# Ending a data-dependent loop over expert slots: an earlier branch, down products inside gate and up, and another waiter for the last scatter

## The reference, cut to what matters

```python
def _moe(h, router_w, router_bias, w_gate, w_up, w_down):
    ...
    _, idx = lax.top_k(masked, TOP_K)
    w = jnp.take_along_axis(scores, idx, axis=-1)
    w = w / jnp.sum(w, axis=-1, keepdims=True)
    comb = jnp.sum(jax.nn.one_hot(idx, N_EXPERTS, dtype=jnp.float32) * w[..., None], axis=1).astype(h.dtype)
    y = jnp.zeros_like(h)
    for e in range(N_EXPERTS):
        he = jax.nn.silu(h @ w_gate[e]) * (h @ w_up[e])
        y = y + comb[:, e:e + 1] * (he @ w_down[e])
    return y

def reference(...):
    for i in range(DEPTH):
        ...
        x = x + g1 * yx
        hx = _rmsnorm(x, norm_ffn[i]) * (1 + sc2) + sh2
        ...
        x = x + g2 * y.reshape(b, l, d)
    return x
```

## Time and profile before

| | us |
|---|---|
| runs before: lowest, median, highest | 1151.88, 1154.61, 1158.58 |
| span of the profiled execution | 1154.3 |
| PE busy | 1078.6 (93% of the span) |
| DVE busy | 802.1 (69%) |
| ACT busy | 480.6 (42%) |
| POOL busy | 178.4 (15%) |
| DMA, mean over the span | 211 GB/s |
| granted TensorE clock, mean | 0.976 of full |

### The profile page before, as it was taken

One profiled execution on the slowest core, in us unless ns is written; L12 is line 12 of the kernel. 1 busy time (PEld: TensorE's weight loads), 2 busy tenths in 40 slices (PEclk: granted clock), 3 DMA queues, 4 the chain that ended last, 5 costly groups with the idle time before them and its releaser, 6 DMA issues.

```text
span 1154.3 us, 14887 instructions
## 1 busy us (share of the span) xinstructions
PE 1078.6 (93%) x4739; PEld 793.5 (69%) x4739; DVE 802.1 (69%) x966; ACT 480.6 (42%) x662; POOL 178.4 (15%) x135
## 2 busy tenths in 40 slices
PE   4999999899999999589999999999999999999992
PEld 2554456577777776268888888878887677777771
DVE  5886996788988887356345435454575788988881
ACT  5211224276676765431111111132232366676760
POOL 2101111122232232100000000000000123323331
PEclk9989999999999999889999999999999899999996
DMA  9878649677979973603733223313134888999742
GB/s 366 316 270 316 255 190 416 226 247 205 330 241 320 342 231 75 238 21 125 273 110 115 74 103 127 127 38 145 73 132 161 342 271 262 353 337 297 227 97 43
DMA packets 82002, 243.48 MB, mean 211 GB/s; under 512 B 10016, under 2 KB 34808, under 8 KB 72700
## 3 DMA queue, kind: packets, MB, share of 16 engines
q1 hardware_dynamic: 62436, 188.88, 43.3%
q0 software_dynamic: 17920, 48.31, 16.5%
q10 hardware_dynamic: 1560, 5.26, 1.3%
HBM read 218.29 MB, written 40.89 MB: 225 GB/s over the span
## 4 chain that ended last, share of the span: by engine, by line
PE 76%; DVE 11%; DMA 6%; issue 3%; ACT 2%; SPq 0%; POOL 0%; DVEq 0%; ACTq 0%; POOLq 0%
PE PS L1944 21%; PE PS L1822 8%; PE PS L2047 7%; PE PS L2051 7%; PE PS L2048 7%; PE PS L1957 6%; PE PS L1963 5%; PE PS L1934 4%; DVE ACC L1133 3%; PE PS L1673 3%; PE PS L1635 2%; DMA WAE<-in_w_ada_dram 2%; PE PS L1837 1%; DMA x_dram<-YO,TOKI 1%; DMA SLAB<-in_w_ada_dram 1%
## 5 line engine op out<-in xcount | busy, mean ns | idle before, releaser
L1454 DVE TENSOR_TENSOR WL<-RAW,WH 128x1024 fp32r<-128x1024 f32 x192 | 225.4, 1216 | 0.2
L927 ACT ACTIVATE WH<-RAW 128x1024 fp32r x184 | 184.6, 1052 | 35.1 <-issue 25.2
L2047 PE MATMUL PS<-HTH,WINH 128*128 128x512 f32 x384 | 150.9, 393 | 5.6 <-DVE HTL L1554 5.3
L1944 PE MATMUL PS<-WH,XTH 128*128 128x512 f32 x368 | 147.3, 400 | 5.5 <-issue 5.5
L2048 PE MATMUL PS<-HTL,WINH 128*128 128x512 f32 x384 | 150.0, 391 | 0.0
L1944 PE MATMUL PS<-WH,XTL 128*128 128x512 f32 x368 | 144.1, 392 | 0.0
L1944 PE MATMUL PS<-WL,XTH 128*128 128x512 f32 x368 | 143.5, 390 | 0.0
L2051 PE MATMUL PS<-HTH,WINL 128*128 128x512 f32 x384 | 118.8, 390 | 0.0
L1957 PE MATMUL PS<-WDR,HETF 128*128 x184 | 87.9, 600 | 5.7 <-DVE YO L1468 4.9
L1468 DVE SCALAR_TENSOR_TENSOR YO<-PS,WOF,ROWS 128x1024 f32<-128x1024 f32 x46 | 59.0, 1284 | 42.3 <-PE PS L1963 35.1
L2047 PEld LDWEIGHTS PS<-HTH,WINH 128*128 128x128 f32 x384 | 72.3, 188 | 22.3 <-DVE HTL L1554 4.8
(11 more groups left out here) (244 smaller groups left out, 1723.7 us busy)
## 6 DMA issues: line engine op xcount, KB each, us to landing
RAW<-in_moe_w_gate_dram SPq DMA_DIRECT2D x32, 1024.0 KB, 6.9
RAW<-in_moe_w_up_dram SPq DMA_DIRECT2D x32, 1024.0 KB, 10.9
WDR<-in_moe_w_down_dram SPq DMA_DIRECT2D x32, 1024.0 KB, 10.0
WA<-in_w_ada_dram SPq DMA_DIRECT2D x28, 1024.0 KB, 7.8
WAE<-in_w_ada_dram SPq DMA_DIRECT2D x12, 1024.0 KB, 8.9
WINR<-in_conv_w_in_dram SPq DMA_DIRECT2D x24, 512.0 KB, 3.9
SLAB<-in_w_ada_dram SPq DMA_DIRECT2D x8, 1024.0 KB, 12.3
X<-x_dram SPq DMA_DIRECT2D x16, 512.0 KB, 5.7
```

The lines of the kernel that those rows point to most:

```text
L927: nc.scalar.activation(piece_of(WH[par], i), raw_piece(at, i), ACT.Copy).then_inc(w_high, 1)
L1454: V.tensor_tensor(piece_of(WL[par], i), raw_piece(e, i), piece_of(WH[par], i).bitcast(f32), ALU.subtract).then_inc(w_low, 1)
L1944: ins = T.matmul(bank(2), x[:, ch, :], w[par][:, :, ch, :], start=ch == 0 and i == 0, stop=ch == NC - 1 and i == 2)
L2047: T.matmul(bank(b), WINH[par][:, ch, :], HTH[:, ch, cols], start=ch == 0, stop=False)
```

## The change

The deciding branch is asked before the last two slots instead of after them. `ending(i, used)` takes the place of `slots_from`: slots 1 to 13 are always run, and if `used > 2 * i`, slots 2i-2 and 2i-1 run in their usual form. Otherwise `closing(2i-2)`, `last(2i-1)` and a `drain` that only evens out the semaphores. In the closing slot TensorE has the down product of slot n-3 between the two halves of gate and up, and in the last slot that of slot n-2. The last slot rounds no weights for a slot that does not come, and prepares its own down weights before its silu. POOL makes two gathers fewer in each layer. The last scatter of a layer counts on a semaphore of its own, `last_scattered`, SyncE waits for that, and POOL waits for no landing after it. Core of the diff, in the order SyncE, POOL, ScalarE (`last`), VectorE (`closing`, `last`), TensorE; `ending` is TensorE's and has the same shape on the other engines:

```diff
-                sp.wait_ge(moe_done, 1)
+                sp.wait_ge(last_scattered, 16)
...
-        sp.wait_ge(moe_done, 2)
+        sp.wait_ge(last_scattered, 32)
...
         def drain(layer, n):
-            scatter(layer, n - 2)
-            scatter(layer, n - 1)
-            pool.wait_ge(y_scattered[layer], 16 * n)
-            for par in range(2):
-                pool.wait_ge(gathered[layer][par], (min(n + 2, MAX_SLOTS) + 1 - par) // 2 * 16)
+            scatter(layer, n - 2, y_scattered[layer])
+            scatter(layer, n - 1, last_scattered)
             pool.sem_inc(y_added, MAX_SLOTS - n + 1)
...
+            def last(s):
+                xt_high(s)
+                down_weights(s - 1)
+                down_high(s, down_loaded(s))
+                gate(s)
+                hidden_high(s)
...
+            def closing(s):
+                before, after = expert_of(s - 1), expert_of(s + 1)
+                xt_low(s)
+                y_evac(s - 2, s % 2)
+                weights_low(s + 1, (s + 1) % 2, after, (0,))
+                het_split(s - 1)
+                down_low(s - 1, before)
+                weights_low(s + 1, (s + 1) % 2, after, (1, 2))
+                y_evac(s - 1, 1 - s % 2)
+                weights_low(s + 1, (s + 1) % 2, after, (3,))
+                gated(s, s % 2)
+
+            def last(s):
+                before, at = expert_of(s - 1), expert_of(s)
+                xt_low(s)
+                het_split(s - 1)
+                down_low(s - 1, before)
+                y_evac(s - 1, 1 - s % 2)
+                down_low(s, at)
+                gated(s, s % 2)
+                het_split(s)
+                y_evac(s, s % 2)
...
+            def gate_up_around_down(s):
+                pe.wait_ge(he_ready, s + b0)
+                hidden_transposes(s - 1, 1 - s % 2)
+                gate_up(s, s % 2, range(NC // 2))
+                down_of(s - 1, expert_of(s - 1))
+                gate_up(s, s % 2, range(NC // 2, NC))
+
+            def closing(s):
+                transposes(s, s % 2, s // 2 + 1)
+                down_of(s - 2, expert_of(s - 2))
+                gate_up_around_down(s)
+
+            def last(s):
+                transposes(s, s % 2, s // 2 + 1)
+                gate_up_around_down(s)
+                at = expert_of(s)
+                pe.wait_ge(he_ready, s + b0 + 1)
+                hidden_transposes(s, s % 2)
+                down_of(s, at)
...
-            def slots_from(i, used):
+            def ending(i, used):
+                if i > LAST_STEP:
+                    slot(2 * i - 2)
+                    closing(2 * i - 1)
+                    last(2 * i)
+                    drain(MAX_SLOTS)
+                    return
                 with pe.If(used > 2 * i):
-                    for s in slots_of(i):
-                        slot(s)
-                    if i < LAST_STEP:
-                        slots_from(i + 1, used)
-                    else:
-                        drain(MAX_SLOTS)
+                    slot(2 * i - 2)
+                    slot(2 * i - 1)
+                    ending(i + 1, used)
                 with pe.Else():
+                    closing(2 * i - 2)
+                    last(2 * i - 1)
                     drain(2 * i)
```

More of the change, by code:

```diff
@@ L655, in gather, with scatter @@
                                     ).then_inc(gathered[layer][par], 16)
-        def scatter(layer, s):
+        def scatter(layer, s, done):
             pool.wait_ge(yo_ready, s + (layer * MAX_SLOTS + 1))
@@ L714, in _ @@
             pool.wait_ge(x_stored[layer], 16 * NT)
-            for s in range(2 * ALWAYS):
+            for s in range(2 * ALWAYS - 2):
                 slot(layer, s)
-            slots_from(layer, ALWAYS, used)
-            pool.sem_inc(moe_done, 1)
+            ending(layer, ALWAYS, used)
             if layer == 0:
@@ L980, in _ @@
             nc.scalar.activation(SG[:], bank(2)[:, 0:FF], ACT.Silu).then_inc(silu_g, 1)
-            for s in range(1, 2 * ALWAYS):
+            for s in range(1, 2 * ALWAYS - 2):
                 slot(s)
-            slots_from(ALWAYS, used)
+            ending(ALWAYS, used)
             if layer == 0:
@@ L1493, in drain, with ending @@
                         dve.sem_inc(sig, MAX_SLOTS - n)
[L1494 to L1504 removed]
+                    dve.sem_inc(w_low, PIECES * (MAX_SLOTS - n))
+            def ending(i, used):
+                if i > LAST_STEP:
+                    slot(2 * i - 2)
+                    closing(2 * i - 1)
+                    last(2 * i)
+                    drain(MAX_SLOTS)
+                    return
+                with dve.If(used > 2 * i):
+                    slot(2 * i - 2)
+                    slot(2 * i - 1)
+                    ending(i + 1, used)
                 with dve.Else():
+                    closing(2 * i - 2)
+                    last(2 * i - 1)
                     drain(2 * i)
@@ L1993, in drain, with ending @@
                         pe.sem_inc(sig, MAX_SLOTS - n)
-            def slots_from(i, used):
-                with pe.If(used > 2 * i):
-                    for s in slots_of(i):
-                        slot(s)
-                    if i < LAST_STEP:
-                        slots_from(i + 1, used)
-                    else:
-                        drain(MAX_SLOTS)
+            def ending(i, used):
+                if i > LAST_STEP:
+                    slot(2 * i - 2)
+                    closing(2 * i - 1)
+                    last(2 * i)
+                    drain(MAX_SLOTS)
+                    return
+                with pe.If(used > 2 * i):
+                    slot(2 * i - 2)
+                    slot(2 * i - 1)
+                    ending(i + 1, used)
                 with pe.Else():
+                    closing(2 * i - 2)
+                    last(2 * i - 1)
                     drain(2 * i)
```

99 lines of the change are left out of this document (45 added, 54 removed).

## The result

| | median us | range us | runs |
|---|---|---|---|
| before | 1155.97 | 1151.88 to 1162.58 | 20 |
| changed | 1161.42 | 1157.38 to 1166.81 | 20 |

The ratio is 1.0046, with a 95% interval of 1.0033 to 1.0058. The change costs about 5.4 us where 2.5 us of gain were forecast. The profiled execution of the changed kernel took 1157.38 us, the lowest of its 20 runs (span 1155.6 us). T is the silu of slot n-3, and times are counted from it as in the prediction.

The account below looks back on a forecast made before the run. TensorE was taken to bound the kernel, with 76% of the chain. Layer 0 at +3.1 and layer 1 at -5.6 gave -2.5 us, 1151.8 on the span of 1154.3, stated as 1152 us; range 1149 to 1155.

Parts of the forecast that it names:

- s: Fetch time of a jump to code not on the engine: taken as 5.3 us in layer 0, 3.5 in layer 1.
- What bounds, and that a jump costs a fetch: Whole kernel and its branches: TensorE holds 76% of the chain; jumping to code not on the engine waits for a fetch.
- Rival C: At the deciding branch: jumps cost nothing, giving 1145.7 us; chance 0.13.
- Start of slot n-2: Behind the deciding branch: gate and up starts at T + s + 2.75, against T + 3.93 in a steady slot.
- TensorE's own jump ... stays hidden behind ACT's: At the deciding branch: TensorE's 3.8 us jump starts some 4 us ahead of its arithmetic, so adds nothing.
- The clock in the ends: Last two slots: no cost for half clock; TensorE's new gap of about 2 us was counted by length.
- From gate and up to the last scatter: From slot n-2's gate and up, at T + s + 2.75, to the last scatter, at T + s + 31.2: 28.45 us.
- Layer 0 behind the scatter: After layer 0's last scatter: SyncE's direct wait saves the step over POOL, -0.3 us; the clock gives -0.7.
- The -0.7 for the clock before the convolution: Before the convolution after layer 0: less TensorE idle time gives back between 0 and -2.8 us; -0.7 taken.
- The barrier, -4.6 us: Closing barrier after layer 1: POOL's fixed 6.89 us overlap the landing, 8.9 us behind the issue instead of 13.5.
- rival B: Closing barrier: waits for the landing, then does its 6.89 us; the 4.6 us are lost, 1156.5 us; chance 0.25.
- Rival D: ACT's exit code: each end pays two fetches, up to 5.3 us more per layer, 1162.5 us; chance 0.10.

Follow-up runs that it names:

- e3: Kernel before with the condition turned round on all four engines, so the exit code stands right behind the branch: 1152.58 us, ratio 0.9964.
- e1: Changed kernel run again with no edit, to profile a more typical execution: 1163.12 us, ratio 1.0052 to the kernel before.
- e9: Changed kernel with the exit code right behind the branch on TensorE alone; the other three engines still jump far: 1168.24 us, ratio 1.0098 to the kernel before.
- e8: Changed kernel with the exit code right behind the branch on ACT, DVE and POOL; TensorE alone jumps far: 1160.64 us, ratio 1.0033 to the kernel before.
- e2: Kernel before with only the wait changed: SyncE waits for the last scatter, POOL for no landing: 1154.00 us, ratio 0.9979.
- e4: Changed kernel with the exit code right behind the branch on all four engines: 1151.57 us, ratio 0.9955 to the kernel before.
- e5: Kernel before with both the exit code right behind the branch and SyncE waiting for the last scatter, old slot order: 1150.33 us, ratio 0.9940.
- e10: Changed kernel with layer 0's two input projection weight loads put behind SyncE's wait for the last slots' conversions: 1162.91 us, ratio 1.0048 to the kernel before.
- e7: e4 with four matmuls of no result in TensorE's gap ahead of the last slot's gate and up: 1157.97 us, ratio 1.0012 to the kernel before.
- e6: Kernel before with only the decision taken two slots sooner, old slot order and POOL's old waits: 1163.73 us, ratio 1.0056.

## Why the prediction was wrong

Forecast were -2.5 us; +5.4 were measured. The mechanism, a fetch on the path, was forecast; three terms of the sum failed: s was too small, the half clock inside the ends was put at nothing, and the barrier's gain was too large. By its own steps:

- **What bounds, and that a jump costs a fetch: right.** e3 shows it by moving the code alone. Rival C (jumps for nothing) is out.
- **Start of slot n-2, `T + s + 2.75`: right in form, s too small; the first step that failed.** Read back from gate and up, s was 6.6 in layer 0 and 3.7 in layer 1 in the changed kernel's profile, and 6.6 and 5.2 in e1, where 5.3 and 3.5 were taken. Against e1 that is 1.3 and 1.7 us too little. I had bounded s by 5.3, the longest seen before. One execution with a jump elsewhere is no upper bound. The lower bound, 2.8 in layer 0, was a misreading: there `HETF` waited for TensorE, so the row does not show when ACT was back; with no far jump at all `HETF` comes only 0.66 us sooner (e3).
- **"TensorE's own jump ... stays hidden behind ACT's": held, but by less than thought.** It grew from 3.8 us to 7.06, and its arithmetic was 2.89 and 1.24 us late. Gate and up still waited for `XTL` in both ends of the changed kernel's profile and in layer 0 of e1; only in layer 1 of e1 did TensorE come last, by 0.6 us. Taking its jump away does not start gate and up sooner in layer 0 (e9). Alone, with the others near, it costs 9 us (e8), of which 5.2 lie in the two ends.
- **The clock in the ends, put at nothing: the second step that failed.** The prediction counted only what a shorter idle stretch before the convolution might give back. In each of e1's ends a stretch at half clock in the last slot cost about 1.6 us. It comes behind the gap of 1.9 us on TensorE, which the prediction had named and priced by its length alone.
- **From gate and up to the last scatter, 28.45 us: right at full clock.** The profile shows 28.5 in layer 0 (441.19 to 469.69) and 28.6 in layer 1; e1, with the half clock, 30.1 and 30.2. That the scatter of layer 1 went at T + 35.0 in the profile, close to the forecast T + 34.7, is the luck of that execution: e1 has T + 38.1.
- **Layer 0 behind the scatter.** The direct wait was put at -0.3 us; from the scatter's issue to the loads of `X` it is 5.9 us (469.69 to 475.59) against 6.4. The -0.7 for the clock before the convolution is not secured: from the scatter to the convolution's transposes it took 25.3 us in the changed kernel's profile and 27.2 in e1, against 25.7 before.
- **The barrier, -4.6 us: the third step that failed, by its size.** e2 measures -2.7, all of the wait's gain. The barrier's 6.89 us are not fixed work: begun right behind the scatter the instruction lasts 10.2 to 10.6 us and ends 4.7 us behind the landing. It lies between the forecast and rival B, which had it end 6.9 us behind the landing.
- **Rival D, the only slow one, named the right kind and the wrong place.** It asked for a second fetch inside ACT's exit code; ACT shows none in the changed kernel. The further stall was TensorE's, at the same branch, and it lay beside ACT's, not behind it.

Laid against e1, the scatters came 2.9 and 3.4 us later than forecast (T + 39.4 and T + 38.1 for T + 36.5 and T + 34.7): 3.0 of these 6.3 us are s, and the rest the half clock. With 1.9 us of the barrier that turns -2.5 into +5.7.

Put together from the runs another way: the old jump cost 4.1 us (e3) and the new one 11.5 (e1 against e4), so the move of the decision is +7.4; the wait is -2.7 (e2) and the order about +1.2 (e4 against e5, not clear of the noise). That makes +5.9, where the two comparisons measured +5.4 and +6.4.

## What to carry to other kernels

Suspect a fetch where an "issue" gap begins at a branch, and test it by moving the code alone (e3). Its price is set by what the engines would be doing meanwhile: put the rare arm right behind the branch, or place the branch where every engine still has queued work. Ask it of each engine apart: the one that is back last sets the start, and the next may be only a microsecond behind it (e10). Price a new gap on TensorE by its length and by the clock behind it. Keep the inline arm short, since the common path now jumps over it (e7).

## What the runs showed of the hardware that was not expected

- The same branch on TensorE's sequencer takes 65 ns in the median and, at its longest, 3.8 us in the kernel before, 7.06 in the changed one and 7.59 in e8.
- Removing one engine's stall can make the whole slower: e9 is 5.1 us above e1 though TensorE's own stall is gone; its idle time is then one stretch of 5.12 us in layer 0 and 4.34 in layer 1, and the work behind it runs at half clock for some us.
- A gap of 1.9 us on TensorE was followed by the half clock in some executions (e1 and e9 in both layers, layer 1 of e4) and not in others (the changed kernel's profile, e8, e10, layer 0 of e4).
- POOL's instruction in the closing barrier took 6.89 us in three kernels in which nothing was in flight at its start (before, e3, e6), and 10.20 to 10.64 us where it started right behind a scatter.
